# Two instruction orders inside a step of difference attention

## The reference

```
s = einsum('bqhmd,bkhmd->bhmqk', q_blk, k) * scale     # m = 0, 1: two maps per head
s = where(mask, s, -inf)
p = softmax(s)
o = einsum('bhmqk,bkhd->bqhmd', p, v)
o = o[..., 0, :] - lam * o[..., 1, :]
o = rmsnorm(o, out_gain) * (1.0 - lam_init)
```

## Time and profile before

| what | value |
|---|---|
| runs of the kernel | 3595.18, 3603.27, 3605.26 us; median 3603.27 |
| the profiled execution's own time | 3603.17 us |
| its span | 3601.8 us |
| busy: TensorE, VectorE, ScalarE | 3413.9, 2082.6, 1329.6 us |
| mean granted TensorE clock | 0.979 of full speed |
| the four passes, first to last maximum | 142 to 230, 393 to 469, 1182 to 1268, 1434 to 1510 us |

### The profile page before, as it was taken

How to read it: one execution, slowest core, us unless ns; L and a number is a source line. 1 busy time by engine, 2 the same in 40 slices (tenths; PEclk the granted TensorE clock), 3 DMA queues, 4 the chain that set the end, 5 groups by cost and what they waited for, 6 DMA issues and landing times.

```text
span 3601.8 us, 55906 instructions
## 1 busy us (share of the span) xinstructions
PE 3413.9 (95%) x23320; PEld 2796.3 (78%) x23320; DVE 2082.6 (58%) x3847; ACT 1329.6 (37%) x2476; POOL 65.5 (2%) x32
## 2 busy tenths in 40 slices
PE   7989999999999889999999999999888989999998
PEld 6767688888888677788888887767677678788887
DVE  6776753544457667644544458664665589674434
ACT  5456543333224456443332323222432234232222
POOL 0000000000000000000000000000000034000000
PEclk9999999999999999999999989999999999999999
DMA  4221123333333211223333332225110323233332
GB/s 135 77 66 48 53 77 106 99 92 96 99 120 95 78 59 48 59 76 117 94 100 94 99 107 79 88 71 163 49 36 19 112 71 122 89 129 100 100 94 88
DMA packets 353825, 315.35 MB, mean 88 GB/s; under 512 B 11348, under 2 KB 281812, under 8 KB 353576
## 3 DMA queue, kind: packets, MB, share of 16 engines
q1 hardware_dynamic: 352712, 309.56, 28.1%
q10 hardware_dynamic: 864, 2.23, 0.2%
HBM read 288.15 MB, written 23.59 MB: 87 GB/s over the span
## 4 chain that ended last, share of the span: by engine, by line
PE 76%; DVE 14%; ACT 5%; issue 3%; DMA 1%; POOL 0%; SPq 0%; DVEq 0%; ACTq 0%; POOLq 0%
PE banks L528 13%; PE banks L529 12%; PE banks L530 12%; PE banks L427 8%; PE banks L429 8%; PE banks L428 8%; DVE weights_r L368 2%; PE banks L3216 2%; PE banks L2622 1%; ACT weights_high_r L361 1%; PE banks L628 1%; PE banks L2608 1%; PE banks L1113 1%; PE banks L1100 1%; ACT probabilities L1249 1%
## 5 line engine op out<-in xcount | busy, mean ns | idle before, releaser
L368 DVE TENSOR_TENSOR weights_r<-weights,weights_high_r 128x1024 fp32r<-128x1024 f32 (+3 forms) x520 | 605.2, 1172 | 379.2 <-ACT weights_high_r L361 378.4
L528 PE MATMUL banks<-h_T_hi,weights_high_r 128*128 128x512 f32 (+2 forms) x1904 | 760.1, 399 | 15.0 <-issue 4.0
L529 PE MATMUL banks<-h_T_lo,weights_high_r 128*128 128x512 f32 (+2 forms) x1904 | 737.3, 387 | 1.7 <-issue 1.7
L530 PE MATMUL banks<-h_T_hi,weights_r 128*128 128x512 f32 (+2 forms) x1904 | 737.8, 387 | 0.0
L361 ACT ACTIVATE weights_high_r<-weights 128x1024 fp32r<-128x1024 f32 (+3 forms) x520 | 510.6, 992 | 361.1 <-DMA weights<-in_w_mlp 213.2
L528 PEld LDWEIGHTS banks<-h_T_hi,weights_high_r 128*128 128x128 f32 x1904 | 362.0, 190 | 104.8 <-issue 32.5
L530 PEld LDWEIGHTS banks<-h_T_hi,weights_r 128*128 128x128 f32 x1904 | 361.4, 190 | 72.9
L529 PEld LDWEIGHTS banks<-h_T_lo,weights_high_r 128*128 128x128 f32 x1904 | 362.1, 190 | 71.5 <-issue 5.9
L427 PE MATMUL banks<-weights_high_r,h_T_hi 128*128 128x512 f32 (+3 forms) x704 | 292.4, 415 | 11.6 <-ACT cellsX L577 6.0
L429 PE MATMUL banks<-weights_high_r,h_T_lo 128*128 128x512 f32 (+3 forms) x704 | 267.4, 380 | 0.0
L428 PE MATMUL banks<-weights_r,h_T_hi 128*128 128x512 f32 (+3 forms) x704 | 267.2, 380 | 0.0
(11 more groups left out here) (571 smaller groups left out, 5469.4 us busy)
## 6 DMA issues: line engine op xcount, KB each, us to landing
weights<-in_w_in SPq DMA_DIRECT2D x182, 512.0 KB, 3.7
weights<-in_w_mlp SPq DMA_DIRECT2D x128, 512.0 KB, 3.8
weights<-in_ffn_w_in SPq DMA_DIRECT2D x44, 512.0 KB, 3.7
weights<-in_w_out SPq DMA_DIRECT2D x24, 512.0 KB, 3.6
weights<-in_ffn_w_down SPq DMA_DIRECT2D x22, 512.0 KB, 3.2
weights<-in_w_mem_kv SPq DMA_DIRECT2D x16, 512.0 KB, 3.6
weights<-in_w_diff_o SPq DMA_DIRECT2D x16, 512.0 KB, 3.8
weights<-in_w_mla_o SPq DMA_DIRECT2D x8, 512.0 KB, 3.3
```

The costliest lines, as they stand in the source:

```text
L368: ve.e.tensor_tensor(self.part(c.w_raw_r, u), self.part(c.w_raw, u), self.part(c.w_high_r, u).bitcast(F32), ALU.subtract).then_inc(*ve.tel ...
L528: pe.e.matmul(out, lhsT=wh[:, k, :], rhs=hi[k][:, cols], start=(k == 0), stop=False)
L529: pe.e.matmul(out, lhsT=wh[:, k, :], rhs=lo[k][:, cols], start=False, stop=False)
L530: mm = pe.e.matmul(out, lhsT=wl[:, k, :], rhs=hi[k][:, cols], start=False, stop=(k == self.chunks - 1))
```

## The change

On VectorE, in a step n, mask and maximum of unit n come first, then the scaling of n-4, then the joining of n-1. On ScalarE the exponentials of n come ahead of the copy of the turned probabilities of n-3. TensorE's order is not touched. Since lines move, the same instructions have new line numbers: the exponentials are at L1240 and the copy at L1249, mask and maximum at L1262 and L1265, the scaling at L1270, the joining at L1276, L1278 and L1281.

```diff
     def act(self):
         for n in range(self.n):
-            if self.unit(n - 3):
-                m, keys = n - 3, self.keys(n - 3)
-                ac.wait_ge("filled", self.tag, "turn", m)
-                if m > 1:
-                    ac.wait_ge("filled", self.tag, "values", m - 2)
-                ...
-                ac.e.activation(c.pT[m % 2][:, 0:keys], c.slots[(self.tag, "turn", m)][:, 0:keys],
-                                ACT.Copy).then_inc(*ac.frees(self.tag, "turn", m))
             if self.unit(n):
                 ac.wait_ge("top", self.tag, n)
                 ...
                 for j in range(2):
                     ac.e.activation(self.p(n, j)[:, 0:keys], c.slots[(self.tag, f"scores {j}", n)][:, 0:keys], ACT.Exp, ...
+            if self.unit(n - 3):
+                ... the same copy
             yield
     def dve(self):
         for n in range(self.n):
+            if self.unit(n):
+                ... mask and maximum, as below
+            if self.unit(n - 4):
+                ... scaling, as below
             if self.unit(n - 1):
                 ... joining
-            if self.unit(n - 4):
-                m = n - 4
-                ve.wait_ge("filled", self.tag, "values", m)
-                ...
-                ve.e.tensor_scalar(self.out(m), ..., self.stat(m)[:, 4:5], None, ALU.mult)
-            if self.unit(n):
-                for j in range(2):
-                    ve.wait_ge("filled", self.tag, f"scores {j}", n)
-                ve.e.tensor_tensor(both[:, :, keys - P:keys], ..., ALU.add).then_inc(*ve.step())
-                ve.settle()
-                ve.e.tensor_reduce(st[:, 0:2], both, AX.X, ALU.max, negate=True).then_inc(*ve.tell("top", self.tag, n))
             yield
```

More of the change, by code:

```diff
@@ L1231, in act @@
         for n in range(self.n):
-            if self.unit(n - 3):
-                m, keys = n - 3, self.keys(n - 3)
-                ac.wait_ge("filled", self.tag, "turn", m)
-                if m > 1:
-                    ac.wait_ge("filled", self.tag, "values", m - 2)
-                else:
-                    ac.wait_all(self.free)
-                ac.e.activation(c.pT[m % 2][:, 0:keys], c.slots[(self.tag, "turn", m)][:, 0:keys],
-                                ACT.Copy).then_inc(*ac.frees(self.tag, "turn", m))
             if self.unit(n):
@@ L1250, in act @@
                                     accum_out=st[:, 2 + j:3 + j]).then_inc(*ac.frees(self.tag, f"scores {j}", n))
+            if self.unit(n - 3):
+                m, keys = n - 3, self.keys(n - 3)
+                ac.wait_ge("filled", self.tag, "turn", m)
+                if m > 1:
+                    ac.wait_ge("filled", self.tag, "values", m - 2)
+                else:
+                    ac.wait_all(self.free)
+                ac.e.activation(c.pT[m % 2][:, 0:keys], c.slots[(self.tag, "turn", m)][:, 0:keys],
+                                ACT.Copy).then_inc(*ac.frees(self.tag, "turn", m))
             yield
@@ L1256, in dve @@
         for n in range(self.n):
+            if self.unit(n):
+                st, keys = self.stat(n), self.keys(n)
+                both = c.score_banks[n % 2][:, :, 0:keys]
+                for j in range(2):
+                    ve.wait_ge("filled", self.tag, f"scores {j}", n)
+                ve.e.tensor_tensor(both[:, :, keys - P:keys], both[:, :, keys - P:keys],
+                                   c.causal[:, :].unsqueeze(1).broadcast_to([P, 2, P]), ALU.add).then_inc(*ve.step())
+                ve.settle()
+                ve.e.tensor_reduce(st[:, 0:2], both, AX.X, ALU.max, negate=True).then_inc(*ve.tell("top", self.tag, n))
+            if self.unit(n - 4):
+                m = n - 4
+                ve.wait_ge("filled", self.tag, "values", m)
+                ve.wait_all(self.free)
+                ve.e.tensor_scalar(self.out(m), c.slots[(self.tag, "values", m)][:, 0:P], self.stat(m)[:, 4:5], None,
+                                   ALU.mult).then_inc(*ve.frees(self.tag, "values", m))
             if self.unit(n - 1):
@@ L1266, in dve @@
                 ve.e.scalar_tensor_tensor(p0, p1, st[:, 6:7], p0, ALU.mult, ALU.add).then_inc(*ve.tell("joined", self.tag, m))
-            if self.unit(n - 4):
-                m = n - 4
-                ve.wait_ge("filled", self.tag, "values", m)
-                ve.wait_all(self.free)
-                ve.e.tensor_scalar(self.out(m), c.slots[(self.tag, "values", m)][:, 0:P], self.stat(m)[:, 4:5], None,
-                                   ALU.mult).then_inc(*ve.frees(self.tag, "values", m))
-            if self.unit(n):
-                st, keys = self.stat(n), self.keys(n)
-                both = c.score_banks[n % 2][:, :, 0:keys]
-                for j in range(2):
-                    ve.wait_ge("filled", self.tag, f"scores {j}", n)
-                ve.e.tensor_tensor(both[:, :, keys - P:keys], both[:, :, keys - P:keys],
-                                   c.causal[:, :].unsqueeze(1).broadcast_to([P, 2, P]), ALU.add).then_inc(*ve.step())
-                ve.settle()
-                ve.e.tensor_reduce(st[:, 0:2], both, AX.X, ALU.max, negate=True).then_inc(*ve.tell("top", self.tag, n))
             yield
```

## The result

The changed kernel ran in 3577.43 us (median of 5 runs, 3573.36 to 3581.93); the kernel before ran in 3595.18 us in the same comparison (5 runs, 3591.09 to 3605.26). The ratio is 0.9942, with a 95% interval of 0.9927 to 0.9956: 0.6% faster, or 21 us of 3600; the two medians lie 17.8 us apart. In later comparisons, with more runs, the kernel before had a median of 3600.7 to 3602.6.

A forecast was written before the change was run, and what follows sets the result against it. TensorE, busy 95% of the span, was taken as the bound, with 41.7 us idle in the four passes in reach. 2 x (-2.9 - 2.0) = -9.8 us, discounted to -8, gave 3595 us; range 3581 to 3609.

The forecast's parts named there:

- the walk through steps 5 to 7: Pass A's three steps with stalls: scores shift by +0.6, +0.1 and -0.8 us; only the last leaves the group.
- the second rival: The late copy decides: values products of 24 units in the passes wait about 0.9 us each, +22 us, 3625; chance 0.10.
- trades places: On VectorE the scaling of n-4 swaps joining against maximum ahead of it: between 0.3 us earlier and 0.6 us later.
- the first rival: In the passes, waits for exponentials and L644 go nearly all as the loop gathers lead: -20 us, 3583; chance 0.17.
- the walk's and pass B's terms: Waits for exponentials and scaling, per layer: pass A -0.8, -0.2, +0.4; pass B -0.9, -0.3, -0.1, +0.6 us.
- Waits for L644: Pass A's four values-product waits for the copy of another stage's turned tile: -0.6, 0, -0.5 and -1.2 us.
- Waits for L656: Pass B: TensorE's wait for VectorE's L656, which is behind L368, gets shorter by 1.3 us.
- The discount of 2 us: The sum over both layers, -9.8 us, was cut to -8 in case a load or bank is late next.
- The clock, counted as zero: Five half-clock stretches in the two passes A cost 8.5 us; their change was counted as zero, +-3.4 us.
- the 1.6 us wait: Pass A, step 7: TensorE's wait before 183.27 moves and shortens from 2.7 to 1.6 us.
- the walk's group: Pass A's three steps with stalls, 5 to 7, taken together: -0.8 us leaves them.

The follow-up runs named there:

- e2: ScalarE's order as changed (exponentials, then copy), VectorE's order as in the kernel before; 3626.18 us, ratio 1.0071 to the kernel before.
- e7: ScalarE's order as changed; VectorE's order scaling, mask and maximum, joining; 3600.54 us, ratio 0.9994 to the kernel before.
- e6: ScalarE's order as in the kernel before; VectorE's order scaling, mask and maximum, joining; 3578.19 us, ratio 0.9935 to the kernel before.
- e1: VectorE's order as changed (mask and maximum, scaling, joining), ScalarE's as in the kernel before; 3568.6 us, ratio 0.9912 to the kernel before.
- e9: Scaling moved to ScalarE, ahead of copy, then exponentials; VectorE does mask and maximum, then joining; 3566.67 us, ratio 0.9891 to the kernel before.
- e10: VectorE's order as changed, ScalarE's as in the kernel before, repeating e1; 3567.94 us, ratio 0.9901 to the kernel before.
- e5: ScalarE's order as in the kernel before; VectorE's order mask and maximum, joining, scaling; 3575.36 us, ratio 0.9928 to the kernel before.

## Why the prediction was right in kind and wrong in size

**Right: what bounds, and where most of the time could come from.** Between the two profiles the gain is TensorE's idle time in the four passes. The loop that was described (exponentials, L361, L368, joining, maximum, exponentials) is the one that mattered: VectorE's order alone gives it all.

**Right: the walk through steps 5 to 7.** The changed profile starts the pass 0.5 us earlier. With that added, the scores that were predicted at 169.5, 176.6 and 182.5 came at 169.5, 176.4 and 182.1. The masks came at 165.6, 171.9 and 178.1 on the same count (165.6, 172.1 and 178.3 predicted). The first two waits for the copy, 1.0 and some 1.8 us by the walk, were 0.83 and 1.59.

**Right: what ScalarE's order costs.** The late copy is a loss by itself: 26 us in `e2` (17.3 us of it idle time in the passes), against the 22 us of the second rival's count (24 places at 0.9 us), and 0.3% beside the changed order of VectorE (4.8 us of idle time).

**Wrong: the part on VectorE, where it says that the scaling "trades places" and counts it as 0.3 us of length.** The sum gave each stall the local shift of one step, as if the maximum always came earlier by just the instructions that were ahead of it. But the scaling has a wait of its own, for the values product of n-4 on TensorE. The trace of before told of it, and the prediction left it out. What that place is worth, `e7` against the changed kernel shows, which differ in it alone: 39.5 against 23.3 us of idle time, ratio 0.9994 against 0.9942, some 19 us. The scaling's line before, asked for what its engine waited for before it (us in total, times):

```profile
  PE banks L1216: 8.9, 11
```

These 8.9 us are not the size of the loss: while the joining stood ahead, it took most of the waiting itself. In `e6` and `e7`, with the joining moved back and the scaling still in front, they are 40.5 and 49.3 us. In pass A, unit 11, TensorE, VectorE and then ScalarE before:

```profile
205.64 1.16 PE L1216 MATMUL banks<-cellsB,cellsS 128*128 128x128 f32 x8 [0.78 <-ACT cellsX L644]
```

```profile
206.83 0.35 DVE L1271 TENSOR_SCALAR cellsA<-banks,softmax_stats 128x128 f32<-128x128 f32 x1 [1.65 <-PE banks L1216]
207.10 0.42 DVE L1278 TENSOR_TENSOR banks<-banks,causal 128x256 f32<-128x256 f32 x1
```

```profile
208.81 0.69 ACT L1249 ACTIVATE probabilities<-banks,softmax_stats 128x512 f32<-128x512 f32 x1 [1.60 <-DVE softmax_stats L1281]
```

The mask of unit 11 stood behind a scaling that waited 1.65 us for TensorE, which itself had waited for L644 on ScalarE. In the changed kernel:

```profile
200.14 1.16 PE L1216 MATMUL banks<-cellsB,cellsS 128*128 128x128 f32 x8 [0.78 <-ACT cellsX L644]
```

```profile
199.60 0.42 DVE L1262 TENSOR_TENSOR banks<-banks,causal 128x256 f32<-128x256 f32 x1
...
201.33 0.35 DVE L1270 TENSOR_SCALAR cellsA<-banks,softmax_stats 128x128 f32<-128x128 f32 x1
```

```profile
201.50 0.69 ACT L1240 ACTIVATE probabilities<-banks,softmax_stats 128x512 f32<-128x512 f32 x1 [1.42 <-PE banks L1224]
```

The mask is at 199.60, ahead of the scaling at 201.33. Against the values product of unit 7 (205.64 before, 200.14 after) it came 1.5 us later before and comes 0.5 us earlier now. The exponentials then waited not for the maximum but for the transposes (L1224) that free their buffer. And in `e7`, where scaling and maximum have changed places back:

```profile
202.91 0.35 DVE L1261 TENSOR_SCALAR cellsA<-banks,softmax_stats 128x128 f32<-128x128 f32 x1 [1.57 <-PE banks L1216]
203.17 0.42 DVE L1268 TENSOR_TENSOR banks<-banks,causal 128x256 f32<-128x256 f32 x1
```

```profile
204.89 0.69 ACT L1240 ACTIVATE probabilities<-banks,softmax_stats 128x512 f32<-128x512 f32 x1 [3.23 <-DVE softmax_stats L1271]
```

the scaling waits 1.57 us, and the exponentials wait 3.23 us for the maximum behind it. So a stall of TensorE passed through the scaling into the next maximum, from there into the exponentials, and with ScalarE's new order into the next copy and back to TensorE. The maximum's release from it lets a lead of VectorE and ScalarE over TensorE carry over from step to step. ScalarE's waits in pass A of the changed kernel show it:

```profile
ACT probabilities L1240 <- DVE softmax_stats L1265: 24.6, 10, 3.8
ACT probabilities L1240 <- PE banks L1224: 8.5, 5, 2.5
```

Five of sixteen exponentials are now held by their buffer and no longer by their maximum, of whose waits 33.9 us became 24.6. Over the four passes the buffer holds 17 of 64 in the changed kernel, 2 in `e7` and none before. This was the first rival: the prediction named the mechanism ("if the shorter loop gathers lead from step to step") and gave it 0.17, with the argument against it that buffers and banks allow no lead above two units and that the copy is now in the loop. The lead stayed within that limit and was enough; the copy took back 4.8 us of idle time (`e1` against the changed kernel).

**The terms that were mis-sized** (idle time, both layers). Waits for exponentials and scaling, 19.3 us before, against those for exponentials, scaling and copy after, 13.6 (and 0.5 for the copy before): -6.2, where the walk's and pass B's terms make -2.6 (-0.8 - 0.2 + 0.4 and -0.9 - 0.3 - 0.1 + 0.6 per layer). Waits for L644: 14.0 to 4.9, so -9.1 against -4.6 (0.6 + 0.5 + 1.2 per layer). Waits for L656: 7.6 to 2.8, -4.8 against -2.6. Each mechanism has the right sign, and each is about twice as large as one step's shift. The discount of 2 us was in the wrong direction as well.

**The clock, counted as zero.** Half-clock stretches in the four passes sum to 17.1 us in both profiles, so by that sum zero was right. But both profiled executions had a mean granted clock of 0.979, and that was the slowest of the changed kernel's five; their mean is 0.981, against 0.980 for the kernel before over the later comparisons. A mean clock higher by 0.001 is some 3.6 us less (an estimate: the time is nearly all TensorE's), so some 4 to 5 us of the gain may be clock. In the other experiments the runs' clock leans the same way: 0.982 in `e1`, `e9` and `e10`, which gain 32, 39 and 36 us with 23 us less idle time each, and 0.978 in `e2`, which loses 26 us with 17 us more. In the profiles the half-clock time in the passes is 10.2, 3.4 and 6.8 us for the first three and 23.9 us for `e2` and for `e7`. So less waiting seems to bring some clock back as well; that this is cause and not chance is not shown, and the half-clock time outside the passes varies by more, from 108 to 148 us, without following the idle time.

Where the stretches lie is not the same in the two profiles. The first two stretches of the changed kernel (columns as in the earlier trace rows):

```profile
176.30:179.70 3.40, 3.40 (x10) 2.72 (x9) 3.30 (x7) 0.38 (x1) 0.00 (x0) 0.50 0.00 0
435.70:442.50 6.80, 5.95 (x16) 4.88 (x17) 1.73 (x3) 2.00 (x5) 0.00 (x0) 0.50 0.01 2
```

Before, the stretch at 184.0 lay behind the last wait of a group; nothing absorbed it, and the way to the next values product (189.72; 186.47 in the changed kernel) was 1.6 us longer than there. Now the stretch at 176.3 lies ahead of the values product at 180.98. The copy for that product ended at 180.9, so without the stretch TensorE would by this count have waited there for as long as it lost; the 1.6 us wait that the prediction had at that place is gone, and the slower clock cost nothing there. The values product of the earlier trace rows shows both:

```profile
193.12 0.91 PE L1216 MATMUL banks<-cellsB,cellsS 128*128 128x128 f32 x6 [1.48 <-ACT cellsX L644]
```

193.12 against 197.01, 3.4 us earlier after the offset of 0.5. Of these 1.2 come from the walk's group (0.8 predicted), 1.6 from the stretch at 184.0 that is gone, and 0.6 from L644, as predicted for it. The 6.8 us in pass B are new, and are one reason why that pass became only 1.3 us shorter for 3.3 us less idle time. Whether the placing of these stretches is chance or an effect of the change stays open.

## What to carry to other kernels

When instructions in an in-order queue trade places, count not only their length but the wait that each brings along: what stood behind a waiting instruction was tied to whatever that one waits for, here a result of the bound engine itself. Here the best place for the instruction that feeds the next round of the loop (the maximum) was the first, with nothing ahead of it that waits for the bound engine. The size of such a wait in the old trace does not price it: it grew from 8.9 to 40 us and more when the other waits ahead of it had gone. Of two reorderings in one change, try each alone: here one gained 0.9 to 1.0% and the other lost 0.3 to 0.7%.

## What the runs showed of the hardware

Over all twelve profiles of this study, TensorE's busy time less half of its half-clock time is 3334 to 3342 us, while the half-clock time goes from 119.5 to 173.7 us. So the same products cost up to 27 us more or less by the clock alone, most of it in parts of the program that no kernel here changes (the passes hold 3.4 to 23.9 us of it). The runs of one kernel show it too: the kernel before took 3592.0 to 3602.4 us at a mean granted clock of 0.982 (seven runs) and 3606.3 to 3609.6 us at 0.977 (three runs). Differences of 0.3% between two versions, as between `e5` (146.3 us of half clock in its profile) and `e1` (127.3), can be of that kind; the idle time of one profile, which came out at 18.5 and 18.4 us for the same order in `e1` and `e10`, told the orders apart better than the ratios did.
